# Norms of a fused two-block model: low parts of a token tile ahead of the next tile's last passes, transposes after the first K block of a product group

## The chip, the cores and the metric

The kernel runs on one core of one Trainium2 chip. The metric is the device time of one launch in microseconds. Before the change three runs gave a median of 2882.7 us (2881.91 to 2884.24).

## What is computed

A forward pass over 512 tokens of width 1024, in fp32, through two blocks. The first has a Mamba-2 layer and a stick-breaking attention layer, each followed by a layer norm, an MLP with squared ReLU and another layer norm. The second has an RWKV-7 mixer beside a sparse attention, and a gated feed-forward, each behind an RMS norm. The parts of the reference that the change touches are the five places where a projection is added to the residual, normed, and fed to the next projection:

```python
h = layer_norm(DEEPNORM_ALPHA * h + mix, ln_mix_g[layer], ln_mix_b[layer])                      # mix1, mix2
h = layer_norm(DEEPNORM_ALPHA * h + squared_relu_mlp(h, ...), ln_mlp_g[layer], ln_mlp_b[layer]) # mlp1, mlp2
u = rmsnorm(h, norm1_g); proj = u @ w_in                                                        # fused with mlp2's norm
h = h + merged @ w_out; z = rmsnorm(h, norm2_g) @ w_ffn_in                                      # norm2
```

## The kernel before, in words

Tokens are held in four tiles t = 0 to 3 of 128. Every fp32 product is made of three passes of TensorE over operands that are split into a high and a low part (high times high, low times high, high times low). POOL (GpSimd) splits each 128x1024 chunk of weights with two instructions, L355 (high) and L357 (low), into a ring of six; the chunk six further on may be split when TensorE has used the one before it in its slot (`split_chunks`).

Around a norm three pieces run at once.

- **The projection** (`Project.tensor`): for the last three K blocks it goes tile by tile, 2 x 3 groups of 6 matmuls of 128x512 (L239) for each token tile: first the column half n = 0, blocks b = 0, 1, 2, then n = 1.
- **The norm** (`Norm`). VectorE (DVE) takes a tile's sums (`stats`, L456 to L467), then the last passes over it: L492 (subtract the mean, times gain), five instructions on one column (`inverse`, L475 to L479) that wait for ScalarE's root (L523), and L495 (times 1/deviation, plus bias). Call the end of these passes norm(t). TensorE then transposes the tile with eight matmuls (`turn(t)`, L425), ScalarE (ACT) copies the high part out of PSUM (`high`, L540 or, with a gain, L543), and DVE subtracts it for the low part (`low_parts`, L443 or L446). In mlp2 a second norm follows the first in each tile (`ln+rms`: ACT's Square at L527, a second `inverse`, L504 into another buffer, which is what is transposed); in norm2 there is only the RMS norm (passes L475 to L479 and L507).
- **The next product** (`Gemm.halves`, L178): the first four column tiles of the next projection are computed in two halves of 256 tokens, s = 0 (tiles 0 and 1) and s = 1 (tiles 2 and 3), for blocks b = 0 to 3 of 24 matmuls each. s = 0 starts when low(1) is made. turn(2) stands after its b = 0 and turn(3) after its b = 2; s = 1 starts when low(3) is made.

So TensorE's queue is: tile 2 of the projection with turn(0) in it, tile 3 with turn(1) in it, halves s = 0 with turn(2) and turn(3) in it, halves s = 1. DVE's queue is stats(t), passes(t), low(t - 1) for t = 1, 2, 3, and low(3). All of it is in program order; there is no scheduler. The last norm of the kernel (`final`) has no transposes and no low parts.

Of the kernel before, what the change touches and what calls it, by code (L numbers as in the profile page):

```python
# [16 lines left out]
NT = SEQ // P  # L17
# [184 lines left out]
class Project:  # L202
# [46 lines left out]
    def tensor(self, pe, x, before=None, norm=None):  # L249


        kit = self.kit
        i = self.chunk0
        for b, (k0, nk) in enumerate(self.head):
            for n in range(2):
                if before is not None and n == 0:
                    before(k0 + nk)

                pe.wait_ge(kit.chunk_split, i + 1)
                for t in range(NT):  # L260
                    if b == 0:
                        self.start_tile(pe, t, n)
                    mm = self.products(pe, x, i, k0, nk, t, n, b == 0, False)
                mm.then_inc(kit.part_used, 1)
                i += 1
        for t in range(NT):
            for n in range(2):
                for b, (k0, nk) in enumerate(self.tail):
                    c = i + n * len(self.tail) + b
                    if t == 0:  # L270
                        if before is not None and n == 0:
                            before(k0 + nk)

                        pe.wait_ge(kit.chunk_split, c + 1)
                    if b == 0 and not self.head:
                        self.start_tile(pe, t, n)
                    last = b == len(self.tail) - 1
                    mm = self.products(pe, x, c, k0, nk, t, n, b == 0 and not self.head, last)
                    if last:
                        mm.then_inc(kit.tile_ready, 1)  # L280
                    elif t == NT - 1:

                        mm.then_inc(kit.part_used, 1)
                if norm is not None and n == 0 and t >= 2:
                    norm.turn(pe, t - 2)

    def wait_tile(self, eng, i):
        eng.wait_ge(self.kit.tile_ready, self.tile0 + i + 1)
# [107 lines left out]
class Norm:  # L396
# [85 lines left out]
    def vector(self, dve):  # L482
        m = self.m
        step = self.kit.vector_chain(dve)
        for t in range(NT):
            ht = m.h[:, t, :]
            self.stats(dve, step, t)
            if t == 0 and self.mode != "rms":

                dve.wait_ge(self.s_rows, self.rows_in)  # L490
            if self.mode in ("ln", "ln+rms"):
                step(dve.scalar_tensor_tensor(out=ht, in0=ht, scalar=m.mv[:, t, 0:1], in1=m.rows[:, 0, :],  # L492
                                              op0=ALU.subtract, op1=ALU.mult))
                r = self.inverse(dve, step, t, 0)
                ins = dve.scalar_tensor_tensor(out=ht, in0=ht, scalar=r, in1=m.rows[:, 1, :], op0=ALU.mult, op1=ALU.add)  # L495
                if self.both:
                    step(ins)
                    dve.engine_nop().then_inc(self.s_sq, 1)

                    dve.wait_ge(self.s_sq, 2 * (self.square0 + t + 1))  # L500
                    dve.tensor_scalar(m.ms[:, t:t + 1], m.mv[:, t, 1:2], 1.0 / D, m.eps[self.eps], ALU.mult, ALU.add)\
                       .then_inc(self.s_var, 1)
                    r = self.inverse(dve, step, t, 1)
                    ins = dve.tensor_scalar(m.unit[:, t, :], ht, r, None, ALU.mult)  # L504
            elif self.mode == "rms":
                r = self.inverse(dve, step, t, 0)
                ins = dve.tensor_scalar(m.unit[:, t, :], ht, r, None, ALU.mult)  # L507
            else:
                r = self.inverse(dve, step, t, 0)
                ins = dve.scalar_tensor_tensor(out=ht, in0=ht, scalar=r, in1=m.rows[:, 0, :], op0=ALU.mult, op1=ALU.mult)  # L510
            ins.then_inc(self.s_norm, 1)
            if t >= 1 and self.final is None:
                self.low_parts(dve, t - 1)
        if self.final is None:
            self.low_parts(dve, NT - 1)

    def scalar(self, act):
        m = self.m

        def root(t):  # L520
            i = self.root0 + self.roots * t
            act.wait_ge(self.s_var, i + 1)
            act.activation(m.std[:, t:t + 1], m.ms[:, t:t + 1], ACT.Sqrt).then_inc(self.s_std, 1)  # L523
            if self.both:
                act.wait_ge(self.s_sq, 2 * (self.square0 + t) + 1)
                junk = self.kit.psum[:, self.gemm.bank(2 * t):self.gemm.bank(2 * t) + 2, :]
                act.activation(junk, m.h[:, t, :].rearrange("p (n c) -> p n c", n=2), ACT.Square,  # L527
                               accum_out=m.mv[:, t, 1:2]).then_inc(self.s_sq, 1)
                act.wait_ge(self.s_var, i + 2)
                act.activation(m.std[:, t:t + 1], m.ms[:, t:t + 1], ACT.Sqrt).then_inc(self.s_std, 1)  # L530

        def high(t):
            if self.final is not None:
                return
            for j in range(2):
                act.wait_ge(self.s_tr, self.turn0 + 2 * t + j + 1)
                dst = m.xin.high[:, 4 * j:4 * j + 4, t * P:(t + 1) * P]
                ps = self.turned(t, j)
                if not self.rms:
                    ins = act.activation(dst, ps, ACT.Copy)  # L540
                else:
                    for q in range(4):
                        ins = act.activation(dst[:, q], ps[:, q], ACT.Copy, scale=m.col(self.gain, 4 * j + q))  # L543
                ins.then_inc(self.s_high, 1)

        root(0)
        root(1)
        for t in range(2, NT):
            high(t - 2)
            root(t)  # L550
        high(NT - 2)
        high(NT - 1)

# [8 lines left out]
def project_norm(nc, kit, m, w, k_tiles, x, alpha, tag, gain=None, mode="ln", eps="ln", late=False):  # L562

    g = Project(kit, w, k_tiles)
    norm = Norm(kit, m, g, alpha, mode, eps, gain)

    def tensor(pe):
        g.tensor(pe, x, norm=norm)

    def vector(dve):  # L570
        if late:
            dve.wait_ge(m.h_landed, 16)
        norm.vector(dve)

    def scalar(act):
        if mode == "ln":
            norm.rows(act, *m.ln_rows[tag])
        norm.scalar(act)

    def gpsimd(pool):  # L580
        kit.split_chunks(pool, g.last_chunk + SPLIT)

    kit.norm = norm
    return tensor, vector, scalar, gpsimd
# [20 lines left out]
def mlp(nc, kit, m, w1, w2, tag, mode="ln", eps="ln", gain=None):  # L605
# [54 lines left out]

    kit.norm = norm
    return tensor, vector, scalar, gpsimd


# [11 lines left out]
def setup(nc, kit, m, a):  # L676
# [52 lines left out]
    def vector(dve):  # L729
        for n in range(2 * NT):  # L730
# [4 lines left out]
                              ALU.subtract).then_inc(s_tf, 1)  # L735

    return tensor, vector, scalar, gpsimd


# [1896 lines left out]
```

## Time and profile before

| | before |
|---|---|
| median of 3 runs | 2882.7 us |
| the profiled execution | 2879.75 us |
| its span, first to last instruction | 2878.0 us |
| TensorE matmuls busy | 2664.6 us (93%) |
| VectorE busy | 1179.6 us (41%) |
| ScalarE busy | 552.7 us (19%) |
| GpSimd busy | 1452.7 us (50%) |
| mean granted TensorE clock | 0.940 of 2.4 GHz |

The profiled execution lies 2.95 us below the median of the runs. Sections of the profile name an instruction by its line; "idle before" is the time in which its engine had nothing to do, with the instruction that ended it.

### The profile page before, as it was taken

To read this page: it belongs to the slowest core of one execution; us is meant where nothing else is said; L and a number is where in the kernel's file an instruction comes from. 1 tells how busy PE (TensorE), PEld (TensorE's weight loads), DVE (VectorE), ACT (ScalarE), POOL (GpSimd) and SP (SyncE) were. 2 spreads that over 40 slices of the span, in tenths; PEclk is the share of its full clock that TensorE was granted. 3 is DMA by queue.
4 is the path that set the end of the run, shared out by engine and by line. 5 is a ranking of instruction groups with operands and counts; after the bars stand their busy time and mean duration, and the time that the engine had idled before them with its cause. 6 is when DMAs were issued, how large, how long until landed. Compare 5 with 4: busy or idle time off the path is not lost.

```text
span 2878.0 us, 32246 instructions
## 1 busy us (share of the span) xinstructions
PE 2664.6 (93%) x13210; PEld 2189.9 (76%) x13210; DVE 1179.6 (41%) x1826; ACT 552.7 (19%) x1103; POOL 1452.7 (50%) x1057
## 2 busy tenths in 40 slices
PE   8998998999999989999999799765899799899998
PEld 6778886888887875588888688554888577788887
DVE  4344764551435003374051663685544312512023
ACT  1113312020110127512020211324222111111010
POOL 7535464575765653366486375100223356366654
PEclk9997999999999999999999899767899799999999
DMA  5221032232332320023232132000000123233322
GB/s 163 74 60 45 29 93 76 81 114 92 96 100 72 107 81 0 29 91 101 67 124 95 54 102 78 1 0 4 1 1 1 48 73 95 72 102 97 88 82 72
DMA packets 104279, 198.89 MB, mean 69 GB/s; under 512 B 9306, under 2 KB 12612, under 8 KB 104132
## 3 DMA queue, kind: packets, MB, share of 16 engines
q1 hardware_dynamic: 101476, 189.36, 21.4%
q10 hardware_dynamic: 2656, 7.47, 0.8%
q8 instruction: 104, 1.70, 0.2%
q14 instruction: 43, 0.35, 0.0%
HBM read 194.71 MB, written 2.10 MB: 68 GB/s over the span
## 4 chain that ended last, share of the span: by engine, by line
PE 82%; DVE 13%; ACT 2%; issue 1%; DMA 0%; SPq 0%; DVEq 0%; ACTq 0%; POOLq 0%; POOL 0%
PE psum L140 32%; PE psum L239 21%; PE psum L142 7%; PE psum L178 4%; PE psum L1925 2%; PE psum L1202 1%; PE psum L1935 1%; PE psum L1193 1%; PE psum L1221 1%; DVE big L1617 1%; DVE best L1616 1%; PE psum L910 1%; DVE big L815 1%; PE psum L1902 1%; PE psum L924 1%
## 5 line engine op out<-in xcount | busy, mean ns | idle before, releaser
L140 PE MATMUL psum<-x_split,weight_split_ring 128*128 128x512 f32 x3984 | 912.9, 391 | 13.6 <-DVEq L2561 13.1
L357 POOL TENSOR_TENSOR weight_split_ring<-weight_ring,weight_split_ring 128x1024 fp32r<-128x1024 f32 (+1 forms) x366 | 876.4, 2395 | 30.6
L140 PEld LDWEIGHTS psum<-x_split,weight_split_ring 128*128 128x128 f32 x3984 | 751.6, 189 | 170.1 <-DVEq L2561 13.3
L355 POOL TENSOR_SCALAR weight_split_ring<-weight_ring 128x1024 fp32r<-128x1024 f32 (+1 forms) x366 | 397.7, 1087 | 851.2 <-PE psum L239 352.4
L239 PE MATMUL psum<-weight_split_ring,hidden_split 128*128 128x512 f32 x2448 | 576.6, 397 | 8.2 <-DVEq L2561 8.2
L239 PEld LDWEIGHTS psum<-weight_split_ring,hidden_split 128*128 128x128 f32 x2448 | 460.5, 188 | 119.8 <-DVEq L2561 8.6
L142 PE MATMUL psum<-weight_split_ring,x_split 128*128 128x512 f32 (+2 forms) x1152 | 254.2, 384 | 1.8 <-DVEq L2561 1.4
L142 PEld LDWEIGHTS psum<-weight_split_ring,x_split 128*128 128x128 f32 x1152 | 215.9, 205 | 40.1 <-DVEq L2561 1.8
L178 PE MATMUL psum<-x_split,weight_split_ring 128*128 128x256 f32 x960 | 129.3, 299 | 28.9 <-DVE x_split L446 18.1
L650 DVE TENSOR_TENSOR big<-big 128x512 f32<-128x512 f32 x64 | 86.5, 1352 | 163.9 <-ACT big L635 163.9
L178 PEld LDWEIGHTS psum<-x_split,weight_split_ring 128*128 128x128 f32 x960 | 125.9, 207 | 31.5 <-DVE x_split L446 19.6
L456 DVE SCALAR_TENSOR_TENSOR residual<-residual,psum 128x512 f32<-128x512 f32 x48 | 32.7, 681 | 255.8 <-PE psum L239 255.8
L2068 POOL TENSOR_TENSOR big<-big,pair_masks 128x512 f32<-128x512 f32 x48 | 60.8, 1270 | 151.0 <-PE psum L1925 92.2
L635 ACT ACTIVATE big<-psum 128x512 f32<-128x512 f32 x64 | 38.3, 598 | 435.2 <-PE psum L140 374.9
L1276 DVE SCALAR_TENSOR_TENSOR big<-psum,big 128x384 f32<-128x384 f32 (+1 forms) x48 | 27.3, 597 | 199.1 <-ACT big L1249 199.1
L652 DVE TENSOR_TENSOR hidden_split<-big,hidden_split 128x512 fp32r<-128x512 f32 x64 | 106.1, 1658 | 2.2
L391 DVE SCALAR_TENSOR_TENSOR residual<-residual,psum 128x512 f32<-128x512 f32 x24 | 16.5, 688 | 213.4 <-PE psum L239 213.4
L2339 DVE TENSOR_TENSOR big<-big,psum 128x512 f32<-128x512 f32 x22 | 15.1, 688 | 194.9 <-PE psum L140 194.9
L239 PE MATMUL psum<-weight_split_ring,x_split 128*128 128x512 f32 x384 | 88.2, 391 | 3.5 <-DVEq L2561 3.5
L239 PEld LDWEIGHTS psum<-weight_split_ring,x_split 128*128 128x128 f32 x384 | 71.8, 188 | 18.7 <-DVEq L2561 4.0
L523 ACT ACTIVATE deviation<-mean_square 128x1 f32<-128x1 f32 x24 | 4.9, 203 | 380.2 <-DVE mean_square L467 380.2
L813 DVE TENSOR_SCALAR big<-psum,parameter_columns 128x512 f32<-128x512 f32 x32 | 25.7, 804 | 119.6 <-PE psum L140 119.6
(351 smaller groups left out, 2996.1 us busy)
## 6 DMA issues: line engine op xcount, KB each, us to landing
weight_ring<-in_mlp_w SPq DMA_DIRECT2D x128, 512.0 KB, 3.6
weight_ring<-in_w_in SPq DMA_DIRECT2D x92, 512.0 KB, 3.6
weight_ring<-in_w_ffn_in SPq DMA_DIRECT2D x40, 512.0 KB, 3.6
weight_ring<-in_w_out SPq DMA_DIRECT2D x24, 512.0 KB, 3.6
weight_ring<-in_w_ffn_out SPq DMA_DIRECT2D x22, 512.0 KB, 3.8
weight_ring<-in_sb_w_q SPq DMA_DIRECT2D x8, 512.0 KB, 3.5
weight_ring<-in_sb_w_k SPq DMA_DIRECT2D x8, 512.0 KB, 3.6
weight_ring<-in_sb_w_v SPq DMA_DIRECT2D x8, 512.0 KB, 3.5
```

The lines of the kernel that those rows point to most:

```text
L140: mm = pe.matmul(out, wp[:, k, m * P:(m + 1) * P], xp, start=first, stop=last)
L142: mm = pe.matmul(out, xp[:, m * P:(m + 1) * P], wp[:, k, 0:n], start=first, stop=last)
L178: mm = pe.matmul(out, wp[:, k, m * P:(m + 1) * P], xp[:, cols], start=first, stop=last, skip_group_check=True)
L239: mm = pe.matmul(out, xp[:, t * P:(t + 1) * P], wp[:, k, :], start=first and k == 0 and q == 0, stop=last and k == nk - 1 and q == 2)
L355: pool.tensor_scalar(part.high[:, 0:nk, 0:n], raw, 1.0, 0.0, ALU.mult, ALU.add).then_inc(self.high_made, 1)
L357: pool.tensor_tensor(part.low[:, 0:nk, 0:n], raw, part.high[:, 0:nk, 0:n].bitcast(F32), ALU.subtract)\
L456: dve.scalar_tensor_tensor(out=hs, in0=hs, scalar=self.alpha, in1=ps, op0=ALU.mult, op1=ALU.add)\
L635: act.activation(m.relu_tmp[:, n % 2, :], ps, ACT.Relu).then_inc(kit.tile_free, 1)
L650: step(dve.tensor_tensor(sq, r, r, ALU.mult))
L652: dve.tensor_tensor(m.hid.low[:, n % HALF, :], sq, m.hid.high[:, n % HALF, :].bitcast(F32), ALU.subtract)\
L1925: mm = pe.matmul(quad(g)[:, q], m.level[:, g, q, :], m.X[d][:, g, q, :], start=True, stop=True)
L2068: pool.tensor_tensor(m.level[:, g], m.kb[:, g], across(m.pair_mask[:, 1 + lv, :], NHP), ALU.mult)\
```

## The change

Three pieces of program order move, and nothing is added or taken away.

```diff
@@ Project.tensor
                     elif t == NT - 1:
 
                         mm.then_inc(kit.part_used, 1)
-                if norm is not None and n == 0 and t >= 2:
-                    norm.turn(pe, t - 2)
+                    if norm is not None and n == 0 and b == 0 and t >= 2:
+                        norm.turn(pe, t - 2)
@@ Norm.vector
             self.stats(dve, step, t)
+            if self.final is None and 1 <= t < NT - 1:
+                self.low_parts(dve, t - 1)
...
             ins.then_inc(self.s_norm, 1)
-            if t >= 1 and self.final is None:
-                self.low_parts(dve, t - 1)
         if self.final is None:
+            self.low_parts(dve, NT - 2)
             self.low_parts(dve, NT - 1)
@@ Norm.scalar
             act.activation(m.std[:, t:t + 1], m.ms[:, t:t + 1], ACT.Sqrt).then_inc(self.s_std, 1)
+
+        def square(t):
+            i = self.root0 + self.roots * t
             if self.both:
...
         root(0)
-        root(1)
-        for t in range(2, NT):
-            high(t - 2)
+        square(0)
+        for t in range(1, NT):
             root(t)
+            if t < NT - 1:
+                high(t - 1)
+            square(t)
         high(NT - 2)
         high(NT - 1)
```

TensorE at mix1, before (L239 is the projection, L425 the transposes, L178 the halves):

```order
L239 MATMUL psum<-weight_split_ring,hidden_split 128x512 x138
L425 MATMUL psum<-constants,residual 128x128 x8
L239 MATMUL psum<-weight_split_ring,hidden_split 128x512 x36
L425 MATMUL psum<-constants,residual 128x128 x8
L239 MATMUL psum<-weight_split_ring,hidden_split 128x512 x18
L178 MATMUL psum<-x_split,weight_split_ring 128x256 x24
```

and after:

```order
L239 MATMUL psum<-weight_split_ring,hidden_split 128x512 x126
L425 MATMUL psum<-constants,residual 128x128 x8
L239 MATMUL psum<-weight_split_ring,hidden_split 128x512 x36
L425 MATMUL psum<-constants,residual 128x128 x8
L239 MATMUL psum<-weight_split_ring,hidden_split 128x512 x30
L178 MATMUL psum<-x_split,weight_split_ring 128x256 x24
```

turn(0) and turn(1) stand twelve matmuls earlier; turn(2) and turn(3), in the halves, stay. (Lines of Norm move by two to four in the changed file.)

DVE at mix1, from the sums of tile 1 on, before:

```order
L461 BN_AGGR mean_variance<-norm_stats 128x2
L467 TENSOR_SCALAR mean_square<-mean_variance,epsilons 128x1
L492 SCALAR_TENSOR_TENSOR residual<-residual,mean_variance,gain_rows 128x1024
L475 RECIPROCAL inverse_deviation<-deviation 128x1
L476 TENSOR_TENSOR deviation<-inverse_deviation 128x1
L477 TENSOR_TENSOR deviation<-deviation,mean_square 128x1
L478 TENSOR_SCALAR deviation<-deviation 128x1
L479 TENSOR_TENSOR inverse_deviation<-inverse_deviation,deviation 128x1
L495 SCALAR_TENSOR_TENSOR residual<-residual,inverse_deviation,gain_rows 128x1024
L443 TENSOR_TENSOR x_split<-psum,x_split 128x4x128 x2
```

and after:

```order
L461 BN_AGGR mean_variance<-norm_stats 128x2
L467 TENSOR_SCALAR mean_square<-mean_variance,epsilons 128x1
L443 TENSOR_TENSOR x_split<-psum,x_split 128x4x128 x2
L494 SCALAR_TENSOR_TENSOR residual<-residual,mean_variance,gain_rows 128x1024
L475 RECIPROCAL inverse_deviation<-deviation 128x1
L476 TENSOR_TENSOR deviation<-inverse_deviation 128x1
L477 TENSOR_TENSOR deviation<-deviation,mean_square 128x1
L478 TENSOR_SCALAR deviation<-deviation 128x1
L479 TENSOR_TENSOR inverse_deviation<-inverse_deviation,deviation 128x1
L497 SCALAR_TENSOR_TENSOR residual<-residual,inverse_deviation,gain_rows 128x1024
```

The low parts (L443) move from behind tile 1's last passes to ahead of them; the same happens at tile 2. At tile 3 the passes come first and low(2) and low(3) follow.

ACT at mlp2, where the norm has two roots and a Square for each tile, before:

```order
L523 ACTIVATE deviation<-mean_square 128x1
L527 ACTIVATE psum,mean_variance<-residual 128x1024
L530 ACTIVATE deviation<-mean_square 128x1
L543 ACTIVATE x_split<-psum,parameter_columns 128x128 x8
```

and after:

```order
L524 ACTIVATE deviation<-mean_square 128x1
L547 ACTIVATE x_split<-psum,parameter_columns 128x128 x8
L531 ACTIVATE psum,mean_variance<-residual 128x1024
L534 ACTIVATE deviation<-mean_square 128x1
```

The copies of high(t - 1) stand between the first root of tile t and its Square, for t = 1 and 2.

## Rows read from the trace of the kernel before

**Rows 1.** Who TensorE waited for, whole span: us in total, times, longest

```profile
PE psum L178 <- DVE x_split L446: 18.1, 2, 15.1
PE psum L178 <- DVE x_split L443: 10.6, 3, 3.6
```

**Rows 2.** Timeline of PE at mix1: start us, us, engine, line, operation [idle before]

```profile
543.44 8.64 PE L239 MATMUL psum<-weight_split_ring,hidden_split 128*128 128x512 f32 x36
...
560.65 4.64 PE L178 MATMUL psum<-x_split,weight_split_ring 128*128 128x256 f32 x24 [3.49 <-DVE x_split L443]
...
565.92 5.99 PE L178 MATMUL psum<-x_split,weight_split_ring 128*128 128x256 f32 x48
571.75 1.05 PE L425 MATMUL psum<-constants,residual 128*128 128x128 f32 x8
```

**Rows 3.** Timeline of DVE at mix1, passes of tile 2, low(1), last pass of tile 3

```profile
549.75 1.82 DVE L492 SCALAR_TENSOR_TENSOR residual<-residual,mean_variance,gain_rows 128x1024 f32<-128x1024 f32 x1
...
555.06 2.27 DVE L479 TENSOR_TENSOR inverse_deviation<-inverse_deviation,deviation 128x1 f32<-128x1 f32 x1
557.37 2.03 DVE L495 SCALAR_TENSOR_TENSOR residual<-residual,inverse_deviation,gain_rows 128x1024 f32<-128x1024 f32 x1
559.32 1.27 DVE L443 TENSOR_TENSOR x_split<-psum,x_split 128x512 fp32r<-128x512 f32 x2
...
569.61 2.04 DVE L495 SCALAR_TENSOR_TENSOR residual<-residual,inverse_deviation,gain_rows 128x1024 f32<-128x1024 f32 x1
```

**Rows 4.** Timeline of POOL at mix1, first of six chunks without a pause

```profile
549.45 1.05 POOL L355 TENSOR_SCALAR weight_split_ring<-weight_ring 128x1024 fp32r<-128x1024 f32 x1 [23.95 <-PE psum L239]
550.59 3.23 POOL L357 TENSOR_TENSOR weight_split_ring<-weight_ring,weight_split_ring 128x1024 fp32r<-128x1024 f32 x1
```

**Rows 5.** Timeline of ACT at mix1, copies of high(1)

```profile
552.56 1.08 ACT L540 ACTIVATE x_split<-psum 128x512 fp32r<-128x512 f32 x2 [2.49 <-PE psum L425]
```

**Rows 6.** Timeline of PE and DVE at mlp1: first 24 halves, norm(3), turn(3)

```profile
924.07 5.46 PE L178 MATMUL psum<-x_split,weight_split_ring 128*128 128x256 f32 x24 [3.48 <-DVE x_split L443]
...
936.00 1.03 PE L425 MATMUL psum<-constants,residual 128*128 128x128 f32 x8
...
933.01 2.03 DVE L495 SCALAR_TENSOR_TENSOR residual<-residual,inverse_deviation,gain_rows 128x1024 f32<-128x1024 f32 x1
```

**Rows 7.** Timeline of PE at mix2: the first 24 halves, turn(3)

```profile
1254.68 5.49 PE L178 MATMUL psum<-x_split,weight_split_ring 128*128 128x256 f32 x24 [3.62 <-DVE x_split L443]
...
1266.84 1.03 PE L425 MATMUL psum<-constants,residual 128*128 128x128 f32 x8
```

**Rows 8.** Timeline of PE at mlp2: turn(3)

```profile
1642.62 1.03 PE L425 MATMUL psum<-constants,big 128*128 128x128 f32 x8
```

**Rows 9.** Timeline of DVE at mlp2: first pass of tile 1, last of tiles 1, 2, 3

```profile
1600.63 1.27 DVE L492 SCALAR_TENSOR_TENSOR residual<-residual,mean_variance,gain_rows 128x1024 f32<-128x1024 f32 x1
...
1606.92 0.75 DVE L504 TENSOR_SCALAR big<-residual,inverse_deviation 128x1024 f32<-128x1024 f32 x1
...
1627.12 1.51 DVE L504 TENSOR_SCALAR big<-residual,inverse_deviation 128x1024 f32<-128x1024 f32 x1
...
1640.03 0.75 DVE L504 TENSOR_SCALAR big<-residual,inverse_deviation 128x1024 f32<-128x1024 f32 x1
```

**Rows 10.** Timeline of ACT at mlp2, copies of high(0)

```profile
1605.83 2.15 ACT L543 ACTIVATE x_split<-psum,parameter_columns 128x128 fp32r<-128x128 f32 x8
```

**Rows 11.** Timeline of PE at norm2: the first 24 halves, turn(3)

```profile
2502.44 4.63 PE L178 MATMUL psum<-x_split,weight_split_ring 128*128 128x256 f32 x24 [2.98 <-DVE x_split L446]
...
2513.53 1.03 PE L425 MATMUL psum<-constants,big 128*128 128x128 f32 x8
```

**Rows 12.** Timeline of DVE at norm2: last pass of tile 2, low(1), last pass of tile 3

```profile
2498.81 1.51 DVE L507 TENSOR_SCALAR big<-residual,inverse_deviation 128x1024 f32<-128x1024 f32 x1
2500.24 2.14 DVE L446 SCALAR_TENSOR_TENSOR x_split<-psum,parameter_columns,x_split 128x128 fp32r<-128x128 f32 x8
...
2509.55 1.51 DVE L507 TENSOR_SCALAR big<-residual,inverse_deviation 128x1024 f32<-128x1024 f32 x1
```

## Prediction

> **What bounds the kernel now.** I read the page first (TensorE 93% busy, no other engine over 50%), then the list of waits, then the timelines of the five norms. The waits [rows 1] say what the change can aim at: the halves (L178) wait five times for low parts, 10.6 us in the three layer norms, 15.1 us in mlp2 and, as the rest of the 18.1, 3.0 us in norm2, together 28.7 us or 1% of the span. The timelines show two things that this list hides.
>
> First, the wait has a tail. Behind it the granted clock falls to the lower of its two levels, 1.2 GHz: the first 24 matmuls of the halves take 4.64, 5.46, 5.49 and 4.63 us [rows 2, 6, 7, 11], against 24 x 0.125 = 3.0 us at the price of the next 48 [rows 2]. That is 2.1 us lost on the mean, 1.6 at the least, 2.5 at the most.
>
> Second, there is another appointment eleven to twelve us later. turn(3) needs norm(3), the last pass over tile 3. At mix1 that pass ends at 569.61 + 2.04 = 571.65 [rows 3], and TensorE starts turn(3) at 571.75 [rows 2]: it arrives on the dot, and no wait is listed. At mlp1 the pass ends at 935.04 and turn(3) starts at 936.00, 1.0 us of slack [rows 6]. So the early wait and its slow clock are spent in time in which DVE has not finished anyway. **What ends last is DVE's chain up to norm(3)**; a gain counts only as far as norm(3) comes earlier.
>
> What sets DVE's pace there is POOL. When TensorE passes tile 3, the six slots of the split ring come free and POOL splits six chunks without a pause from 549.45 on [rows 4]. An L479 on one column takes 2.27 us and L495 takes 2.03 [rows 3], where a pass over all 1024 columns without POOL beside it takes 1.27 (L492 of a tile 1), and L504 takes 0.75 without and 1.51 with POOL [rows 9]. They wait for POOL's instruction to end, and POOL's in turn waits for theirs (L357 took 3.23 us behind L492, others 2.4) [rows 3, 4]. The low parts, which read PSUM, and the sums of a new tile aren't stretched.
>
> **The change at mix1, step by step.** Twelve matmuls earlier is 12 x 8.64/36 = 2.9 us, so turn(1) starts near 549.1 instead of 551.9; norm(1), at 544.0, is there. ACT takes tile 2's root at about 549.9, then copies high(1) for 1.1 us [rows 5]. DVE ends tile 2's sums at 549.75 [rows 3], waits 0.9 us for the first copy and makes low(1) by 552.0, where it made it from 559.32 to 560.6 before. The wait of 3.49 us in front of the halves goes: they start when the projection ends, at 560.65 - 3.49 = 557.16.
>
> Then tile 2's passes. L492 is issued at 552.0 instead of 549.75, 2.25 us late. POOL's first L355 ends at 550.5, its first L357 at 553.0 (2.4 us, nothing in its way). L492 follows and ends at 554.0; L476 waits for the second L355 (to 555.0), L479 for the second L357 (to 557.4), L495 for the third L355 (to 558.5) and ends at 559.55. Before it ended at 557.37 + 2.03 = 559.40. The late start is swallowed, because either way the passes leave behind the same instruction of POOL. Tile 3's sums take 3.1 us, to 562.65; its passes go behind the fourth L355, the fourth L357, the fifth pair and the sixth L355, as before, and **norm(3) is at 571.7 instead of 571.65**.
>
> TensorE: 24 matmuls to 560.1, turn(2) without a wait (norm(2) at 559.6), 0.8 us for it, 48 matmuls in 5.8, at turn(3) by 566.7. There it waits 5.1 us, longer than the wait that went, and the clock drop now falls behind turn(3), with 120 matmuls still to come and no appointment left that hides it. Mix1: 0.0 + 2.1 = **+2.1 us**.
>
> **The other norms.** Mlp1 and mix2 have the same pattern of rows, and norm(3) again 0.1 us later. Their turn(3) starts with norm(3) instead of after it. In mlp1 that gives 0.96 - 0.1 = 0.8 us. For mix2, 11.0 us from the start of the halves to norm(3) as in the two others [rows 2, 3, 6] makes 1265.7 against 1266.84, so 1.0 us [rows 7]. With the clock: **+1.3 and +1.1 us**.
>
> Mlp2 is where the order costs DVE most. Tile 1's sums are done at 1600.63 [rows 9]. Now high(0) comes first: 2.15 us on ACT [rows 10], and low(0), half a copy behind and as long, ends at 1604.2; the passes start 3.6 us late. Their length is 1607.67 - 1600.63 = 7.0 us, to 1611.3, and the end of the second inverse meets POOL's L357: 1612.8 by the pattern of rows 3. turn(1), now due at 1607.6, waits 5.2 us for it, in the middle of tile 3 of the projection, which so ends near 1622.3 instead of 1615.6. Tile 2: sums to 1615.9, high(1) and low(1) to 1619.3, passes against POOL to 1634.3 (they took 15.9 us before from 1612.8; I take 15.0), where norm(2) was at 1628.63 [rows 9]. turn(2) waits for that and hides TensorE's own delay. From norm(2) to norm(3) it was 1640.78 - 1628.63 = 12.15 us; without low(1), 2.1 to 2.3 us, in between, it is 9.9, so norm(3) and turn(3) stand at 1644.2 against 1642.62 [rows 8]: **+1.6 us**. Whether TensorE arrives at turn(3) with a wait long enough for a second clock drop is open; I count none.
>
> Norm2: low(1), 2.14 us [rows 12], moves ahead of the passes of tile 2, and these fall behind one instruction of POOL more: norm(2) at 2503.8 instead of 2500.32. From there to norm(3) it took 10.7 us with low(1) in it. Without that it is 8.6 us, or 10.0 with one more POOL instruction in the way: norm(3) at 2512.4 or 2513.8. I take the second, since tile 2's row of L479 shows such a wait as the common case [rows 3]: turn(3) 0.3 us later than 2513.53 [rows 11], behind a wait of 3 us, and the clock: **+2.4 us**. The other end is -1.1 + 1.6 = +0.5.
>
> Sum: 2.1 + 1.3 + 1.1 + 1.6 + 2.4 = **+8.5 us**. The profiled execution would go from 2879.75 to 2888.3; it lies 2.95 below the median of the runs, and the median goes from 2882.7 to 2891.2. Moves that I count at nothing: turn(0), whose norm(0) is made before it is due; DVE's wait for high(0) at tile 1 in the three layer norms (some 1 us and low(0)'s 1.2), covered by its idle time before the second sum of tile 2, and, if that cover were gone, added to norm(2); ACT's order, since ACT is 19% busy. No DMA is issued in another place, and the chunks of the halves are freed in s = 1 as before.
>
> **Where the skill bears.** Rows 3 and 4 show DVE and POOL alternating. The Trainium skill (SBUF — State Buffer, Who interferes with whom) calls their shared port pair an exclusive lock that is held for the whole instruction. By that rule the outcome is a matter of which instruction asks first, so that a shift of 0.1 us can cost a whole instruction of POOL; the waits of 2.27 and 2.03 us agree. The sum above is one course of that race, and a slip of that kind is the second rival.
>
> **Rivals.** *The clock isn't lost* (chance 0.12). The stall behind 72 matmuls at full pace leaves no slow stretch. Then 4 x 2.1 us go: +0.1 us, 2882.8. Against it: all four waits of 3.0 to 3.6 us had it, and the new ones at mix1, mlp1 and mix2 are 5 us.
>
> *A norm slips behind one POOL instruction more* (0.14). Each costs up to 2.4 us; in three norms 7 us: 2898. For it: in new phases a one-column instruction can miss its gap, as in mlp2 and norm2.
>
> *DVE leaves POOL's stretch earlier* (0.12): faster. With low(1) ahead, a gap opens for two more of the passes, and norm(3) comes before TensorE. This decides at mix1, mlp1 and mix2: were norm(3) there at 566.7, the whole 5.0 us and the clock drop would be won, three times 5.0 = 15 us, less the 4.0 of mlp2 and norm2: 2871.7. From 3 us earlier in each it passes 0.2%. Against it: the passes of tiles 2 and 3 hold ten instructions that wait for POOL, and POOL's six chunks end near 573.9 in any case.
>
> *Little moves* (0.10): the losses are real but half as large, and the slack of mlp1 and mix2 pays for them, 2885.
>
> **Chances and range.** The forecast has 0.52. About 0.2% or 5.8 us is what a measurement of this kernel can tell from no change. Slower by more: forecast 0.48 of its 0.52 (the rest is a clock loss at its lower bound with +0.5 in norm2), and the slip 0.14: 0.62. Faster by more: 0.10. Within: 0.28. The range leaves out most of the faster case and the worst slips: from 2881.5 (no clock loss, norm2 at its low end) to 2897.0 (2.5 us of clock four times, +1.6, and one or two slips).
>
> **What would show it.** After: the waits of the halves for low parts gone at all places but perhaps mlp2; L425 waiting for L495 (now L497) 5.1 us in each layer norm; turn(3) at 571.8 at mix1; the first 24 matmuls behind it near 5 us instead of 2.9; a wait of some 5 us at turn(1) and 8 to 9 at turn(2) in mlp2. It is wrong if norm(3) comes over 1 us before 571.7, or if the matmuls behind the new waits keep 0.125 us.

## The result and the profile after

| | before | after |
|---|---|---|
| median | 2883.85 us (7 runs, 2880.0 to 2887.33) | 2893.46 us (7 runs, 2891.08 to 2896.53) |
| ratio after/before | | 1.0034, 95% interval 1.0022 to 1.0046 |
| the profiled execution, its span | 2879.75, 2878.0 us | 2891.92, 2890.2 us |
| mean granted TensorE clock | 0.940 | 0.937 |

The changed kernel is slower by 9.6 us (6.3 to 13.3 by the interval); 8.5 us were forecast. The waits of TensorE in the norms, which were all at L178 [rows 1], are at the transposes now (L425), but for one of 0.2 us in mlp2, in the list of waits after (us in total, times, longest):

```profile
PE psum L425 <- DVE big L506: 15.7, 3, 8.9
PE psum L425 <- DVE residual L497: 15.3, 3, 5.2
PE psum L425 <- DVE big L509: 4.7, 2, 3.2
```

That is 35.7 us of waiting in eight places (three each in mlp2 and over the layer norms, two in norm2) instead of 28.7 in five. No low part is waited for before the halves begin: the change did what it says. The page's chain of work that ended last goes through DVE for 15% of the span, after 13% before. This says what the path runs through and not what was lost, as 2% of the span would be 58 us:

```profile
PE 81%; DVE 15%; ACT 2%; issue 1%; SPq 0%; DMA 0%; DVEq 0%; ACTq 0%; POOLq 0%; POOL 0%
```

TensorE at mix1 after the change (the timeline; start, us, line, tiles, count, idle before), which answers to [rows 2]:

```profile
539.11 1.03 PE L425 MATMUL psum<-constants,residual 128*128 128x128 f32 x8
...
549.17 7.24 PE L239 MATMUL psum<-weight_split_ring,hidden_split 128*128 128x512 f32 x30
556.25 3.04 PE L178 MATMUL psum<-x_split,weight_split_ring 128*128 128x256 f32 x24
559.13 1.03 PE L425 MATMUL psum<-constants,residual 128*128 128x128 f32 x8
559.92 6.00 PE L178 MATMUL psum<-x_split,weight_split_ring 128*128 128x256 f32 x48
570.98 1.97 PE L425 MATMUL psum<-constants,residual 128*128 128x128 f32 x8 [5.06 <-DVE residual L497]
572.60 16.54 PE L178 MATMUL psum<-x_split,weight_split_ring 128*128 128x256 f32 x120
588.98 11.30 PE L140 MATMUL psum<-x_split,weight_split_ring 128*128 128x512 f32 x49
```

Three more lines of the kernel before belong beside these:

```profile
542.65 1.04 PE L425 MATMUL psum<-constants,residual 128*128 128x128 f32 x8
...
572.56 14.64 PE L178 MATMUL psum<-x_split,weight_split_ring 128*128 128x256 f32 x120
587.03 13.34 PE L140 MATMUL psum<-x_split,weight_split_ring 128*128 128x512 f32 x58
```

The halves follow the projection without a wait, and the first 24 take 3.04 us, not 4.64: both gains are real. Then TensorE stands 5.06 us before turn(3), and the slow clock comes behind it: eight transposes take 1.97 us instead of 1.05, and 16.38 us pass until L140 begins, for 120 matmuls that took 14.47 us before. The granted clock reads 1.00 over the 48 matmuls before the wait, 0.50 from turn(3) to 575.0, and 1.00 again from 577.6 on. This place lies 0.74 us earlier in this execution than in the other (turn(0) began at 542.65, or 539.85 at its new place 2.8 us ahead, and begins at 539.11 now), so turn(3) at 570.98 is 571.72 on the old scale. It was 571.75.

DVE in the same stretch, which answers to [rows 3], and POOL's first instructions there [rows 4]:

```profile
549.85 1.29 DVE L443 TENSOR_TENSOR x_split<-psum,x_split 128x512 fp32r<-128x512 f32 x2 [0.75 <-ACT x_split L544]
551.06 2.27 DVE L494 SCALAR_TENSOR_TENSOR residual<-residual,mean_variance,gain_rows 128x1024 f32<-128x1024 f32 x1
...
554.65 2.07 DVE L479 TENSOR_TENSOR inverse_deviation<-inverse_deviation,deviation 128x1 f32<-128x1 f32 x1
556.76 2.04 DVE L497 SCALAR_TENSOR_TENSOR residual<-residual,inverse_deviation,gain_rows 128x1024 f32<-128x1024 f32 x1
...
568.89 2.03 DVE L497 SCALAR_TENSOR_TENSOR residual<-residual,inverse_deviation,gain_rows 128x1024 f32<-128x1024 f32 x1
```

```profile
548.71 1.05 POOL L355 TENSOR_SCALAR weight_split_ring<-weight_ring 128x1024 fp32r<-128x1024 f32 x1 [23.95 <-PE psum L239]
549.84 2.40 POOL L357 TENSOR_TENSOR weight_split_ring<-weight_ring,weight_split_ring 128x1024 fp32r<-128x1024 f32 x1
552.21 2.03 POOL L355 TENSOR_SCALAR weight_split_ring<-weight_ring 128x1024 fp32r<-128x1024 f32 x1
```

L443 waits 0.75 us for ACT's copy and now comes first, so tile 2's passes start 2.1 us later than before (551.06, or 551.80 on the old scale, against 549.75). They end at 558.80, or 559.5 on the old scale, against 559.40. L494 waits for POOL's first L357, which ends at 552.24; before, L492 waited for the first L355 and L357 waited for it (3.23 us against 2.40 here). DVE and POOL have changed places in one turn of their alternation, and the rest follows as before.

Mlp2, where DVE's idle time could not take the new order:

```profile
1602.06 1.03 PE L425 MATMUL psum<-constants,big 128*128 128x128 f32 x8
...
1616.58 1.97 PE L425 MATMUL psum<-constants,big 128*128 128x128 f32 x8 [5.07 <-DVE big L506]
...
1638.62 1.97 PE L425 MATMUL psum<-constants,big 128*128 128x128 f32 x8 [8.85 <-DVE big L506]
1640.24 6.73 PE L178 MATMUL psum<-x_split,weight_split_ring 128*128 128x256 f32 x48
1648.70 1.10 PE L425 MATMUL psum<-constants,big 128*128 128x128 f32 x8 [1.74 <-DVE big L506]
```

One wait of 15.12 us is now three, 15.66 us together. The one before was this:

```profile
1630.75 5.41 PE L178 MATMUL psum<-x_split,weight_split_ring 128*128 128x256 f32 x24 [15.12 <-DVE x_split L446]
```

DVE shows the cause of the first, low(0) behind a wait for its copy (idle 1.30 us) ahead of tile 1's passes:

```profile
1605.76 2.16 DVE L446 SCALAR_TENSOR_TENSOR x_split<-psum,parameter_columns,x_split 128x128 fp32r<-128x128 f32 x8 [1.30 <-ACT x_split L547]
1607.83 1.28 DVE L494 SCALAR_TENSOR_TENSOR residual<-residual,mean_variance,gain_rows 128x1024 f32<-128x1024 f32 x1
...
1613.35 1.81 DVE L476 TENSOR_TENSOR deviation<-inverse_deviation 128x1 f32<-128x1 f32 x1
```

To compare kernels norm by norm, whatever an execution is ahead or behind elsewhere, I take the stretch from the start of turn(0) to the first L140 behind the halves, less 2.8 us where turn(0) stands twelve matmuls earlier. At mix1 that is 587.03 - 542.65 = 44.4 us before and 588.98 - 539.11 - 2.8 = 47.1 after. Each row is one profiled execution, in us; the sums are taken before rounding:

| kernel | mix1 | mlp1 | mix2 | mlp2 | norm2 | sum | against before |
|---|---|---|---|---|---|---|---|
| before | 44.4 | 45.2 | 45.3 | 57.1 | 44.3 | 236.3 | |
| after | 47.1 | 46.7 | 46.4 | 59.6 | 47.0 | 246.7 | +10.5 |
| 1: transposes alone | 44.4 | 45.2 | 45.2 | 57.1 | 44.3 | 236.2 | -0.1 |
| 2: order of DVE and ACT alone | 48.7 | 49.1 | 46.9 | 59.6 | 45.9 | 250.1 | +13.9 |
| 3: before, POOL's part cut | 39.1 | 39.1 | 38.8 | 48.6 | 39.5 | 205.2 | -31.1 |
| 4: after, POOL's part cut | 39.1 | 39.1 | 38.7 | 50.4 | 39.5 | 206.9 | -29.3 |
| 5: after, TensorE kept busy | 44.5 | 44.5 | 44.2 | 59.6 | 44.7 | 237.5 | +1.2 |
| 6: before, scalar forms | 39.1 | 39.1 | 38.9 | 53.3 | 39.5 | 209.9 | -26.3 |
| 7: after, scalar forms | 40.3 | 40.2 | 40.0 | 59.1 | 39.5 | 219.1 | -17.2 |
| 8: transposes early, scalar forms | 39.1 | 39.1 | 38.8 | 53.3 | 39.5 | 209.9 | -26.4 |

The two spans differ by 12.2 us. 10.5 of them lie in these five places; 1.7 lie in the rest, which no part of the change touches, and are less than what executions of one kernel differ by. The way up to mix1, which no edit of the experiments reaches, varies by more than that: put at its old place, turn(0) of mix1 begins between 541.9 and 550.5 us in these ten executions. So the stretches are the finer measure of what each edit does, and the medians the measure of the kernels' times.

### The profile page after: what moved, and what is told of

It is laid out like the page before. It is cut to its first block, busy times and chain, and to the rows that moved or that the text cites. A ratio compares the mean times of both kernels' runs of the same rounds, so it can differ in the third digit from the quotient of the medians.

```text
span 2890.2 us, 32246 instructions
## 1 busy us (share of the span) xinstructions
PE 2672.8 (92%) x13210; PEld 2197.0 (76%) x13210; DVE 1182.2 (41%) x1826; ACT 552.2 (19%) x1103; POOL 1450.6 (50%) x1057
## 4 chain that ended last, share of the span: by engine, by line
PE 81%; DVE 15%; ACT 2%; issue 1%; SPq 0%; DMA 0%; DVEq 0%; ACTq 0%; POOLq 0%; POOL 0%
PE psum L140 32%; PE psum L239 21%; PE psum L142 7%; PE psum L178 3%; PE psum L1931 2%; PE psum L1208 1%; PE psum L1941 1%; PE psum L1199 1%; PE psum L1227 1%; DVE big L1623 1%; DVE best L1622 1%; PE psum L916 1%; DVE inverse_deviation L479 1%; DVE big L821 1%; PE psum L1908 1%
## 5 line engine op out<-in xcount | busy, mean ns | idle before, releaser
L140 PE MATMUL psum<-x_split,weight_split_ring 128*128 128x512 f32 x3984 | 912.8, 391 | 13.6 <-DVEq L2567 13.1
L357 POOL TENSOR_TENSOR weight_split_ring<-weight_ring,weight_split_ring 128x1024 fp32r<-128x1024 f32 (+1 forms) x366 | 876.3, 2394 | 30.6
L140 PEld LDWEIGHTS psum<-x_split,weight_split_ring 128*128 128x128 f32 x3984 | 751.2, 189 | 170.4 <-DVEq L2567 13.3
L355 POOL TENSOR_SCALAR weight_split_ring<-weight_ring 128x1024 fp32r<-128x1024 f32 (+1 forms) x366 | 395.6, 1081 | 863.3 <-PE psum L239 358.5
L239 PE MATMUL psum<-weight_split_ring,hidden_split 128*128 128x512 f32 x2448 | 578.0, 397 | 8.2 <-DVEq L2567 8.2
L239 PEld LDWEIGHTS psum<-weight_split_ring,hidden_split 128*128 128x128 f32 x2448 | 461.5, 189 | 120.4 <-DVEq L2567 8.6
L178 PE MATMUL psum<-x_split,weight_split_ring 128*128 128x256 f32 x960 | 126.2, 295 | 0.2 <-DVE x_split L446 0.2
L178 PEld LDWEIGHTS psum<-x_split,weight_split_ring 128*128 128x128 f32 x960 | 124.3, 203 | 0.8 <-DVE x_split L446 0.4
L239 PE MATMUL psum<-weight_split_ring,x_split 128*128 128x512 f32 x384 | 88.3, 390 | 3.5 <-DVEq L2567 3.5
L239 PEld LDWEIGHTS psum<-weight_split_ring,x_split 128*128 128x128 f32 x384 | 71.8, 188 | 18.8 <-DVEq L2567 4.0
```

What stands on the lines that cost most here:

```text
L140: mm = pe.matmul(out, wp[:, k, m * P:(m + 1) * P], xp, start=first, stop=last)
L178: mm = pe.matmul(out, wp[:, k, m * P:(m + 1) * P], xp[:, cols], start=first, stop=last, skip_group_check=True)
L239: mm = pe.matmul(out, xp[:, t * P:(t + 1) * P], wp[:, k, :], start=first and k == 0 and q == 0, stop=last and k == nk - 1 and q == 2)
L355: pool.tensor_scalar(part.high[:, 0:nk, 0:n], raw, 1.0, 0.0, ALU.mult, ALU.add).then_inc(self.high_made, 1)
L357: pool.tensor_tensor(part.low[:, 0:nk, 0:n], raw, part.high[:, 0:nk, 0:n].bitcast(F32), ALU.subtract)\
```

## The experiments

**1. The transposes alone.** The kernel before, with the first hunk of the change:

```diff
-                if norm is not None and n == 0 and t >= 2:
-                    norm.turn(pe, t - 2)
+                    if norm is not None and n == 0 and b == 0 and t >= 2:
+                        norm.turn(pe, t - 2)
```

> The kernel before with the first piece of the change alone: turn(0) and turn(1) twelve matmuls earlier, the order of DVE and ACT as before. Theory (DVE's chain up to norm(3), paced by POOL, decides): no instruction of that chain moves, low(1) stays behind tile 2's passes, so the halves still wait 3.5 us for it in the layer norms and 15 us in mlp2, turn(3) still starts at its old place; 0 us against before, between -2 and +2. Rival 1 (the earlier transposes are what costs): about +9 us. Rival 2 (the earlier transposes are the good part, spoiled by the order of DVE): 5 us or more faster.

Measured: 2882.85 us against 2883.45 (ratio 1.0000, 0.9992 to 1.0009). The waits for low parts stand as before, in the list of waits:

```profile
PE psum L178 <- DVE x_split L446: 17.9, 2, 14.9
PE psum L178 <- DVE x_split L443: 10.6, 3, 3.6
```

Rivals 1 and 2 both fall. Alone, the earlier transposes neither cost nor bring anything; the high and low parts behind them are held up by DVE's own order.

**2. The order of DVE and ACT alone.** The changed kernel with that hunk taken back.

> The changed kernel with the transposes put back behind the third K block: the order of DVE and ACT alone. Theory: low(0) ahead of tile 1's passes now waits for transposes that come 2.9 us later than in the changed kernel, but the chain meets the same instructions of POOL, so norm(3) comes at most one such instruction later; the loss of the changed kernel is there: +8 to +14 us against before, with L425 waiting for the last pass of tile 3 in all five norms and the clock drop behind it. Rival 1 (the transposes cost): 0 us.

Measured: 2895.17 us, ratio 1.0044 (1.0030 to 1.0057), that is +12.7 us (the medians differ by 11.7): the whole loss is here. The interval overlaps that of the changed kernel, but the stretches add up to 3.4 us more: the earlier transposes help this order in the layer norms, by 1.6, 2.4 and 0.5 us, while norm2 is 1.1 us shorter without them. At mix1 DVE waits 3.36 us for high(0) here and 0.76 there. That moves one wait more to the transposes, and turn(2) waits too:

```profile
559.47 3.04 PE L178 MATMUL psum<-x_split,weight_split_ring 128*128 128x256 f32 x24
565.55 1.09 PE L425 MATMUL psum<-constants,residual 128*128 128x128 f32 x8 [3.03 <-DVE residual L497]
566.40 7.48 PE L178 MATMUL psum<-x_split,weight_split_ring 128*128 128x256 f32 x48
576.93 1.97 PE L425 MATMUL psum<-constants,residual 128*128 128x128 f32 x8 [3.05 <-DVE residual L497]
```

The orders of DVE and ACT were not tested apart. In mlp2 they can't be: with ACT's order of before, low(0) would wait for a copy that stands behind tile 1's Square, and the Square waits for the passes that stand behind low(0).

**3. Before, with POOL's work in the norms cut.** For the six chunks behind each projection:

```diff
             _, _, nk, _, n = self.chunks[i]
+            if i in self.light:
+                n = 8
...
+    kit.light.update(range(g.last_chunk, g.last_chunk + SPLIT))
```

> The kernel before, but POOL splits only the first 8 of 512 columns of the six chunks that it splits during each of the five norms (the rest of these weights is left out, the slots keep older values). Theory (POOL paces DVE's passes): passes of tiles 2 and 3 take as long as those of tile 1, so low(1) is made before the projection ends in the layer norms and norm(3) before TensorE comes to turn(3). In the layer norms the wait of 3.5 us and the slow clock go: turn(3) at 566.7 instead of 571.75 at mix1, 5 to 6 us each; norm2 5 us; mlp2 the 6 to 9 us of its passes' stretching. 27 to 34 us faster than before. Rival (the passes of the last two tiles are slow for another reason, as waits on ScalarE or on themselves): within 3 us of before.

Measured: 2850.2 us, ratio 0.9895 (0.9881 to 0.9908), -30.3 us by the ratio and -33.3 by the medians. The passes of tile 2 have the times of a tile with no POOL beside it (the columns of DVE's timeline as above; the file's lines are three further down, L482 is L479):

```profile
557.61 1.29 DVE L495 SCALAR_TENSOR_TENSOR residual<-residual,mean_variance,gain_rows 128x1024 f32<-128x1024 f32 x1
...
559.70 0.16 DVE L482 TENSOR_TENSOR inverse_deviation<-inverse_deviation,deviation 128x1 f32<-128x1 f32 x1
559.90 1.28 DVE L498 SCALAR_TENSOR_TENSOR residual<-residual,inverse_deviation,gain_rows 128x1024 f32<-128x1024 f32 x1
```

They take 3.6 us instead of 9.7. Of TensorE's five waits for low parts only mlp2's is left, at 6.3 us.

**4. After, with the same cut.**

> The changed kernel with the same part of POOL's splits left out. Theory: no wait at turn(2) or turn(3) in the layer norms, so it is level with the kernel before under the same cut in four norms, and slower only in mlp2, where high(0) and low(0) still stand ahead of tile 1's passes and hold up turn(1): 2 to 5 us slower than the kernel before with the same cut, 24 to 31 us faster than the kernel before. Rival (the loss has nothing to do with POOL and stays whole): 9 to 12 us slower than the kernel before with the same cut.

Measured: 2855.28 us, ratio 0.9906 (0.9893 to 0.9920). The two intervals overlap, so the medians, 5.1 us apart, don't tell 3 from 4. The stretches do: the same to 0.1 us in four norms, and 1.8 us longer in mlp2, where turn(1) and turn(3) wait 3.42 and 3.25 us. I expected 2 to 5 there. So 1.8 of the 5.1 us are explained, and no profile shows more. The reason holds: **where POOL hardly runs, the changed order costs nothing in the layer norms and in norm2**.

**5. After, with TensorE kept busy at the wait.** Products of no use go into a PSUM bank that turn(3) overwrites:

```diff
+                if s == 0 and b == 2 and not norm.both:
+                    norm.gemm.wait_free(pe, 7)
+                    w0 = kit.split_ring[self.chunk0 % SPLIT]
+                    for _ in range(22 if norm.rms else 40):
+                        pe.matmul(kit.psum[:, norm.gemm.bank(6), 0:half], w0.high[:, 0, 0:P], x(0).high[:, 0:half],
+                                  start=True, stop=True, skip_group_check=True)
```

> The changed kernel with matmuls of no use (40 of 128x256 at the layer norms, 22 at norm2, none at mlp2) put in front of turn(3) as soon as tile 3's sums have been read, so that TensorE works while norm(3) is made. Theory: the time of the waits is no loss against the kernel before, the slow clock behind them is. turn(3) starts where it does in the changed kernel, and the 8 transposes and the 120 matmuls behind it keep the full clock: 2.7 us less at each of the four places, 8 to 11 us faster than the changed kernel and within 3 us of the kernel before. Rival (the loss is later norms, not the clock): no faster than the changed kernel, +9 us or more.

Measured: 2885.35 us, ratio to before 1.0007 (0.9999 to 1.0016), 8.1 us below the median of the changed kernel, whose interval of 1.0022 to 1.0046 lies wholly above this one. At mix1:

```profile
569.03 4.96 PE L189 MATMUL psum<-x_split,weight_split_ring 128*128 128x256 f32 x40
574.33 1.09 PE L431 MATMUL psum<-constants,residual 128*128 128x128 f32 x8 [0.34 <-DVE residual L503]
575.18 14.63 PE L178 MATMUL psum<-x_split,weight_split_ring 128*128 128x256 f32 x120
589.65 10.62 PE L140 MATMUL psum<-x_split,weight_split_ring 128*128 128x512 f32 x46
```

turn(3) still waits for norm(3), but behind it the full clock is there (1.00 granted from 574.3 on): 14.47 us for the 120 matmuls, and 2.6, 2.2, 2.2 and 2.3 us less at the four places. Doing useless work is 8 us faster than waiting. Over these four places the waits themselves were no loss against the kernel before (177.9 us of stretches against 179.1); their tails were. Mlp2, which has no such work, keeps its 2.5 us.

**6. Before, with scalar forms.** The three products of the inverse:

```diff
-        step(dve.tensor_tensor(w, r, r, ALU.mult))
-        step(dve.tensor_tensor(w, w, ms, ALU.mult))
+        step(dve.tensor_scalar(w, r, r, None, ALU.mult))
+        step(dve.tensor_scalar(w, w, ms, None, ALU.mult))
         step(dve.tensor_scalar(w, w, -0.5, 1.5, ALU.mult, ALU.add))
-        step(dve.tensor_tensor(r, r, w, ALU.mult))
+        step(dve.tensor_scalar(r, r, w, None, ALU.mult))
```

> The kernel before with the three one-column products of the inverse written with their second factor as the per-partition scalar of a TENSOR_SCALAR, as L467 has it, instead of a TENSOR_TENSOR with two inputs. Nothing is left out. Theory (what waits for POOL is an instruction with two inputs from SBUF): L476, L477 and L479 fall from up to 2.3 us to about 0.2 us each, only the long passes still wait; the 3.5 us waits of the halves go and norm(3) comes before TensorE in the layer norms: 5 to 6 us there each, 5 in norm2, 3 to 8 in mlp2: 20 to 32 us faster than before. Rival (any DVE instruction on SBUF waits for POOL): within 3 us of before.

Measured: 2858.28 us against 2883.5, 25.2 us less, ratio 0.9915 (0.9902 to 0.9929). DVE at tile 2 of mix1, with POOL splitting beside it as ever:

```profile
556.17 0.22 DVE L476 TENSOR_SCALAR deviation<-inverse_deviation 128x1 f32<-128x1 f32 x1
556.42 0.21 DVE L477 TENSOR_SCALAR deviation<-deviation,mean_square 128x1 f32<-128x1 f32 x1
...
556.86 0.21 DVE L479 TENSOR_SCALAR inverse_deviation<-inverse_deviation,deviation 128x1 f32<-128x1 f32 x1
557.11 2.16 DVE L495 SCALAR_TENSOR_TENSOR residual<-residual,inverse_deviation,gain_rows 128x1024 f32<-128x1024 f32 x1
```

The one-column instructions no longer wait; the long pass does. That is enough for the layer norms and norm2, whose stretches are as short as with POOL's work cut.

**7. After, with the same forms.**

> The changed kernel with the same three instructions written with a scalar. Theory: the chain of DVE is short here too, yet in mlp2 turn(1) still waits for high(0) and low(0) ahead of tile 1's passes, and the layer norms keep a small wait at turn(3): slower than the kernel before with the same edit by 4 to 10 us. Rival (with POOL's waits gone the changed order is the better one, since low(1) is ready sooner): equal to or faster than the kernel before with the same edit.

Measured: 2866.1 us, ratio 0.9942 (0.9929 to 0.9954), 7.8 us above the sixth. The stretches add up to 9.1 us: 5.8 in mlp2, and 1.1 in each layer norm, where turn(3) still waits up to 1.0 us. In mlp2 TensorE stops three times again:

```profile
1600.43 1.97 PE L425 MATMUL psum<-constants,big 128*128 128x128 f32 x8 [4.31 <-DVE big L506]
...
1618.13 1.97 PE L425 MATMUL psum<-constants,big 128*128 128x128 f32 x8 [4.35 <-DVE big L506]
...
1630.68 1.97 PE L425 MATMUL psum<-constants,big 128*128 128x128 f32 x8 [3.64 <-DVE big L506]
```

So the order is the worse one with long waits on POOL and with short ones.

**8. Transposes early, DVE's order as before, scalar forms.**

> The kernel before with the earlier transposes (the first piece of the change) and the three scalar forms. Theory: the transposes are never what ends last, so it is within 2 us of the kernel before with the scalar forms alone, 20 to 32 us faster than the kernel before. Rival (with a short chain of DVE the transposes come to bind, as norm2's wait for high(0) suggests): 2 to 4 us faster than without them.

Measured: 2855.88 us, ratio 0.9901 (0.9886 to 0.9916), the lowest median of the kernels here that compute everything. The interval overlaps the sixth's, and every stretch is the same to 0.1 us, so the 2.4 us between their medians aren't to be put down to the transposes.

## Why the prediction was right, and where its sizes were off

The time came out 9.6 us longer against 8.5 forecast, inside the range, and by the mechanism that was forecast. The range was wide, from 1.2 us faster to 14.3 us slower, so what carries the forecast is the agreement norm by norm. Of the 10.5 us in the stretches 2.0 weren't forecast. Point by point, with starts put on the old scale by turn(0):

- **"What ends last is DVE's chain up to norm(3)."** turn(3) was worked out as 571.8, 935.2, 1265.8, 1644.2 and 2513.8. It came at 571.7, 935.1, 1265.7, 1645.0 and 2513.9. Experiments 1 and 2 put all of the loss on the order of that chain.
- **"The late start is swallowed."** At mix1 the passes of tile 2 end 0.1 us later after starting 2.1 us later. Experiments 3 and 4 show why that is: without POOL there is nothing to swallow it, and nothing to lose either.
- **The clock.** This term was undersized: 2.1 us a place, from the cost of the first 24 matmuls of the halves before. Behind the new waits it was 2.7, 2.3, 2.3 and 2.4 us, of which 0.8 are the eight transposes, which stand first now and which the rows of before could not show at the lower clock. Together that is 1.3 us of the 2.0. Experiment 5 is the direct test of this term.
- **Mlp2.** The steps were right one by one: turn(1) at 1612.8 as worked out, turn(2) at 1634.9 against 1634.3, turn(3) at 1645.0 against 1644.2. Of these 0.8 us 0.5 come from tile 2's passes against POOL, which took 15.5 us where 15.0 were chosen, a choice that no row of before decides. No slow stretch followed the last wait of 1.74 us, as counted.
- **Norm2.** The choice of one more instruction of POOL held: turn(3) 0.4 us later than before, 0.3 counted. It was in part luck: the reason given was one row at mix1, and the other end, which would have made this norm 1.9 us cheaper, was as open.
- **The rivals.** The clock was lost at all four places; no norm slipped by a further instruction of POOL; DVE didn't leave POOL's stretch early. That third rival does happen once the inverse no longer waits for POOL, but then the kernel before gains more than the changed one (experiments 6 and 7).

What stays open: why the slow stretches differ. Waits of 2.98 to 3.62 us had shorter and longer ones in the kernel before. In experiment 2, eight transposes behind waits of 3.03 to 3.17 us took 1.09 us three times and 1.93 or 1.97 three times. So 2.1 or 2.4 us a place is a mean over places and no price of a wait of a given length.

## What to carry to other kernels

Before removing a wait, find the next appointment of the engine behind it: if what it meets there comes no earlier, the wait only moves, and here it took TensorE's slow clock with it, to a place where nothing hid it. Work that is moved ahead of a chain that ends last should be ready when its turn comes; here DVE waited 0.75 to 1.30 us each time for ACT's copies, at the head of the chain that decided. When one-column instructions take 2 us, look at what the neighbouring engine runs: writing three of them with a scalar operand was worth 25 us, where shuffling the order cost 10.

## What the runs showed of the hardware that was not expected

A product of two columns as TENSOR_TENSOR took up to 2.27 us beside POOL's splits, and as TENSOR_SCALAR with the second column as its scalar 0.21 or 0.22 us, also beside them; over 1024 columns the TENSOR_SCALAR L504 was stretched all the same, from 0.75 to 1.51 us [rows 9]. I had used the first half of this as a guess in experiment 6.

The Trainium skill (SBUF — State Buffer, Who interferes with whom) names two SBUF inputs and the two-port modes (in which DVE also takes the port pair that it shares with GpSimd) as what contends with GpSimd. That fits all three numbers if a scalar operand doesn't count as an input and only the long TENSOR_SCALAR runs in such a mode; no run here shows the mode.

And the transposes feel the clock as the products do: in the changed kernel eight took 1.97 us behind every wait of 3.16 us or more, and 1.03 to 1.10 elsewhere.
